# Hybrid SSD and gMLP diffusion step on one Trainium2 core: GpSimd casts the four upper parts of a weight tile first, then subtracts the four lower parts

## The reference: what is computed

```python
def _layer(x, mod, h0, lw, rows):
    ...
    h = rms_norm(x, norm_w) * (1 + scale[:, None]) + shift[:, None]
    proj = h @ w_in
    xbc_raw, z_m, dt_raw, u_raw, v_raw, z_g, gl_m, gl_g = jnp.split(
        proj, _split_points(IN_SIZES), axis=-1)
    y_m, h_fin = _ssd_branch(xbc_raw, dt_raw, z_m, h0, conv_w, conv_b, dt_bias, a_log,
                             d_skip, ssm_norm_w, rows)
    y_g = _gmlp_branch(u_raw, v_raw, z_g, sgu_ln_w, sgu_ln_b, w_sp, b_sp)
    merged = jax.nn.sigmoid(gl_m) * (y_m @ w_out_m) + jax.nn.sigmoid(gl_g) * (y_g @ w_out_g)
    return x + gate[:, None] * (merged @ w_out), h_fin
```

## Time and profile before

| what | value |
|---|---|
| median of 3 runs | 1401.03 us (1400.89 to 1401.64) |
| the profiled execution, its own time | 1401.26 us |
| its span in the trace | 1399.5 us |
| PE busy | 1387.0 us, 99% of the span |
| POOL busy | 1029.1 us, 74% of the span |
| DVE busy | 1027.1 us, 73% of the span |
| ACT busy | 467.1 us, 33% of the span |

### The profile page before, as it was taken

One profiled execution on the slowest core, in us unless ns is written; L12 is line 12 of the kernel. 1 busy time (PEld: TensorE's weight loads), 2 busy tenths in 40 slices (PEclk: granted clock), 3 DMA queues, 4 the chain that ended last, 5 costly groups with the idle time before them and its releaser, 6 DMA issues.

```text
span 1399.5 us, 27040 instructions
## 1 busy us (share of the span) xinstructions
PE 1387.0 (99%) x10101; PEld 1331.1 (95%) x10101; DVE 1027.1 (73%) x1503; ACT 467.1 (33%) x1039; POOL 1029.1 (74%) x1421
## 2 busy tenths in 40 slices
PE   8999999999999999999999999999999999999997
PEld 5899999999999999999998999999999999999997
DVE  6988679665677688999978766976566776869234
ACT  5432123214766333001252323241266661320122
POOL 3789886696554499998869898657765546979763
PEclk9999999999999999999999999999999999999999
DMA  9362665123766555444334455722346665453222
GB/s 366 126 151 76 191 167 159 61 66 127 188 179 192 177 204 212 150 151 155 106 136 122 107 165 149 192 86 61 106 135 191 193 173 201 139 190 120 76 76 91
DMA packets 198047, 206.85 MB, mean 148 GB/s; under 512 B 76592, under 2 KB 163760, under 8 KB 196784
## 3 DMA queue, kind: packets, MB, share of 16 engines
q1 hardware_dynamic: 116000, 155.13, 35.6%
q10 hardware_dynamic: 81936, 50.16, 12.4%
HBM read 179.23 MB, written 26.02 MB: 147 GB/s over the span
## 4 chain that ended last, share of the span: by engine, by line
PE 98%; DVE 1%; DMA 0%; SPq 0%; issue 0%; ACT 0%; DVEq 0%; ACTq 0%
PE acc L718 79%; PE X L684 5%; PE acc L684 3%; PE X L972 2%; PE X L952 2%; PE X L988 1%; PE X L1013 1%; PE acc L866 1%; PE X L981 1%; DVE p_lo L1606 1%; DMA ada_pre<-in_wada 0%; DVE ssq L1581 0%; PE X L825 0%; DVE xr L2143 0%; PE X L910 0%; PE acc L732 0%
## 5 line engine op out<-in xcount | busy, mean ns | idle before, releaser
L617 POOL CAST w_hi<-w_st 128x256 fp32r<-128x256 f32 x696 | 410.5, 604 | 337.1 <-PE acc L718 162.2
L621 POOL TENSOR_TENSOR w_lo<-w_st,w_hi 128x256 fp32r<-128x256 f32 x696 | 645.0, 936 | 0.0
L718 PE MATMUL acc<-h_hi,w_hi 128*128 128x320 f32 x1696 | 402.1, 318 | 0.0
L718 PE MATMUL acc<-h_lo,w_hi 128*128 128x320 f32 x1696 | 386.3, 309 | 0.0
L718 PE MATMUL acc<-h_hi,w_lo 128*128 128x320 f32 x1696 | 386.2, 309 | 0.0
L718 PEld LDWEIGHTS acc<-h_hi,w_hi 128*128 128x128 f32 x1696 | 284.4, 188 | 14.7 <-issue 11.8
L718 PEld LDWEIGHTS acc<-h_hi,w_lo 128*128 128x128 f32 x1696 | 283.5, 188 | 0.0
L718 PEld LDWEIGHTS acc<-h_lo,w_hi 128*128 128x128 f32 x1696 | 283.4, 188 | 0.0
L1824 DVE SCALAR_TENSOR_TENSOR cv<-raw,convw_sb,cv 128x642 f32<-128x642 f32 x128 | 137.2, 1072 | 4.5
L1540 DVE SCALAR_TENSOR_TENSOR ada_acc<-ada_st,sc,ada_acc 128x512 f32<-128x512 f32 x112 | 107.8, 1002 | 1.8
L1280 ACT ACTIVATE cvt<-cv 128x642 f32<-128x642 f32 x32 | 23.8, 744 | 158.1 <-DVE cv L1824 158.1
(11 more groups left out here) (264 smaller groups left out, 2322.5 us busy)
## 6 DMA issues: line engine op xcount, KB each, us to landing
w_st<-in_wts SPq DMA_DIRECT2D x174, 512.0 KB, 3.7
cum_bc<-cum_dram ACTq DMA_DIRECT2D x80, 256.0 KB, 5.0
ada_st<-in_wada SPq DMA_DIRECT2D x34, 512.0 KB, 4.3
ex_bc<-ex_dram ACTq DMA_DIRECT2D x64, 128.0 KB, 3.1
ada_pre<-in_wada SPq DMA_DIRECT2D x14, 512.0 KB, 8.9
xs<-xs_dram SPq DMA_DIRECT2D x64, 80.0 KB, 3.8
mga_dram<-c_buf SPq DMA_DIRECT2D x16, 320.0 KB, 5.2
xf<-xf_dram SPq DMA_DIRECT2D x4, 1280.0 KB, 7.1
```

Source lines behind the costliest of these rows:

```text
L617: nc.gpsimd.tensor_copy(quarter(w_hi, slot, q), quarter(w_st, slot, q)).then_inc(s_pool, 1)
L621: nc.gpsimd.tensor_tensor(quarter(w_lo, slot, q), quarter(w_st, slot, q), f(quarter(w_hi, slot, q)), ALU.subtract).then_inc(w_split, 1)
L718: last = mm(a[:, hf, 0:n1], w[:, s, cols], x[:, k, hf * HALF:hf * HALF + n1], start=(k == 0 and n == 0), stop=(k == KC - 1 and n == 2))
```

## The change

In GpSimd's loop the casts are no longer interleaved with the subtractions. Before, quarter q+1 was cast just ahead of the subtraction of quarter q; now all four quarters are cast and then all four are subtracted. The instructions, their operands and the counts on which the subtractions wait are the same.

```diff
         with pool.Fori(1, DEPTH * NT // 2) as i:
             for slot in range(2):
                 split(slot, 16 * i + 16, 2 * i + slot - 1)
-                split_hi(slot, 0)
                 for q in range(WQ):
-                    if q + 1 < WQ:
-                        split_hi(slot, q + 1)
+                    split_hi(slot, q)
+                for q in range(WQ):
                     split_lo(slot, q, 2 * WQ * i + (base + WQ * slot + q + 1))
```

## The result

The changed kernel takes 1403.32 us in the median of 20 runs, the kernel before 1401.17 us in 20 runs beside them. The ratio is 1.0016 with a 95% interval of 1.0010 to 1.0022: 2.15 us or about 0.16% slower. That is inside the 0.2% that the prediction called hard to tell from no change, and with 20 runs each it can be told.

What follows compares the result with a forecast made beforehand. PE's own stream was taken to bound the kernel, with GpSimd nowhere the bound. Waits of 0.43 + 0.13 + 0 + 0 = 0.56 us on the median 1401.03 gave 1401.6 us, range 1400.3 to 1403.5.

Steps and rivals of the forecast that it cites:

- the signs that it had set: In the changed trace: PE waits naming w_lo near 536 and 543 us, 0.3 to 0.7 us; mean split under 0.3 longer.
- PE bounds the kernel, and nothing can be gained: From 35 to 1391 us PE's gaps total 0.09 us; faster by over 0.2% (1398 us or less) had chance 0.03.
- What the order does to the four subtractions: First subtraction of a tile ends two casts later (0.7 to 1.9 us), second one cast; third, fourth unchanged; v tiles untouched.
- The waits at tiles 64 and 65: Near 536 and 543 us PE waits for late first subtractions, 0.43 and 0.13 us, together 0.56 us.
- Tiles 58 and 146, "just in time": First subtractions end 0.12 and 0.07 us ahead of PE's weight loads, so no wait; by the port rule 0.1 at 146.
- The rival "DVE is slowed": Last ym_lo ahead of tile 66: eight instructions at 0.35 us more, 2.8 against 7 us of room; no chance of its own.
- the high end: Waits at tiles 64, 65, 58, 146 of 0.56, 0.70, 1.65, 1.10 us, together 4.0; the range's end 1403.5 us.
- the second rival: Tiles 58 and 146 also wait: with the 0.56, 1.6 to 2.7 us; 1402.3 to 1403.8 us; chance 0.12.

Runs made afterwards that it cites:

- half_104_115: Changed kernel, but in tiles 104 to 115 each subtraction is cut into two of 128 columns: 1401.70 us against 1401.19 for the kernel before.
- alt_92_147: Changed kernel, but with casts and subtractions alternating as before for tiles 92 to 147: 1401.66 us against 1401.19 for the kernel before.
- double_58_146: Changed kernel, but one subtraction per two quarters in tiles 58, 59, 146 and 147: 1404.33 us against 1401.23 for the kernel before.
- grp_104_115: Kernel before, with casts grouped ahead of subtractions only for tiles 104 to 115: 1402.64 us against 1401.27 for the kernel before.
- alt_104_115: Changed kernel, but alternating casts and subtractions as before for tiles 104 to 115: 1402.09 us against 1401.27 for the kernel before.
- late_grouped: Changed kernel with PE's burst for unit 5 two chunks later in its tile: 1401.78 us against 1401.27 for the kernel before.
- its control: Kernel before (alternating) with PE's burst for unit 5 two chunks later: 1401.19 us against 1401.27 for the kernel before.

## Why the prediction was right, and where it was wrong

The sign and the range were right; the forecast of 1401.6 us was 1.7 us short, the loss was 2.15 us where the sum had 0.56, and its reason was not what happened. Of the signs that it had set, the mean split kept its length (5.85 us in both) and the time moved by less than 2.8 us, but between 35 and 1392 us no wait of a matmul names the subtraction: the only one listed is the 1.4 us at the burst.

- **PE bounds the kernel, and nothing can be gained: right for the time.** No variant is faster than the kernel before beyond its interval. The 0.09 us of gaps in PE was not all, though: the burst of unit 5 hid a wait of 0.26 us, and half_104_115, where DVE is early enough, gave back 0.3 us at that place.
- **What the order does to the four subtractions: right for the first, not quite for the third.** In its logic lo2 ends when it did. Counted from the start of its split it does in the mean over the 174 tiles (0.02 us earlier), but for single tiles it moves by 1.4 us forward to 2.0 us back. The DVE instructions that the eight meet are others, and in v tile 103, which had 0.32 us of room before its first matmul, it cost 0.34 us. The forecast left the v tiles out, "although they are the ones in which PE comes closest behind GpSimd", by counting instructions and not their turns with DVE. That this step goes with the alternating order is shown by alt_92_147; which DVE instruction made it was only read from the timeline (GpSimd's four subtractions take 3.42 us there beside `ex` and `xo` on DVE).
- **The waits at tiles 64 and 65, 0.43 and 0.13 us: they did not come.** The step that failed is "I take the tiles' own rows, since DVE's list is the same and is pinned to PE's tiles as before". The timelines of GpSimd and of DVE beside tile 64 in the changed kernel:

```profile
530.99 2.03 POOL L617 CAST w_hi<-w_st 128x256 fp32r<-128x256 f32 x4
532.98 5.16 POOL L621 TENSOR_TENSOR w_lo<-w_st,w_hi 128x256 fp32r<-128x256 f32 x4
```

```profile
534.89 1.36 DVE L1580 TENSOR_TENSOR ssq<-ssq,c_buf 128x640 f32<-128x640 f32 x1
```

  The split began 0.7 us earlier (530.99, before 531.68), and its four casts took 2.03 us, not 1.93 + 0.95 + 0.82: the last three are free, at 0.40 us each from 531.92 us on, where DVE is at an instruction that takes 0.82 us in both kernels (`c_buf<-c_buf,acc`). The first subtraction was done at about 534.3, not 536.66, and PE came at 536.4. DVE paid instead: the instruction at 534.89 started at 533.27 in the kernel before and took 1.01. There DVE has 7 us to spare before tile 66.
- **Tiles 58 and 146, "just in time": right in kind.** Tile 58 did not wait and tile 146 waited 0.16 us, for 0.07 us of room. The Trainium skill's rule that a two-input DVE instruction and GpSimd take turns ("SBUF — State Buffer", "Who interferes with whom"), by which the text had 0.1 us there, came closer than the rows alone. The way of pricing a late quarter holds: double_58_146 was expected to add 0.9 to 1.1 us to the changed kernel and added 0.95 by the medians.
- **The rival "DVE is slowed" was the cause, and it was given no chance.** The forecast had the mechanism right, word for word: DVE "now waits for a subtraction (0.70) where every second one waited for a cast (0.35)". It looked for its price at one place only, the last `ym_lo` ahead of tile 66, and found 7 us of room. The step that failed for the time as a whole is this one: the lateness of DVE was held against one hand-over only. It did not ask where else DVE hands something to PE with no room. That place was in the trace, at 897.80 against 897.91 us, and in the list of waits it is invisible. The runs with one part alone (grp_104_115, +1.4 us), one part undone (alt_104_115, 0.8 left), and the wait taken away with everything else kept (late_grouped, 0.5 left against 0.0 for its control) show this place to be worth 1.3 of the 2.15 us. The same burst in layer 0 is worth 0.35 more by the traces.
- **The range held by luck.** Its bounds were built for first quarters, and DVE's lateness happened to have a size that fell into them, 0.18 us under the high end. That end was itself added up too high. The high end and the second rival add tile 58's wait to those of tiles 64 and 65, but from tile 58's first cast to 549 us GpSimd waits for nobody, so a PE that is late since tile 58 would have found tile 64 ready. Without this the high end is 1.65 + 1.10 = 2.75 us in place of 4.0, and the second rival 1.1 to 2.2 us in place of 1.6 to 2.7. A range that took in 2.2 us would have ended at 1403.2, short of the 1403.32 measured. (The rival's 1402.3 us doesn't follow from its 1.6 either, which gives 1402.6.)

Why DVE meets more subtractions is shown in its numbers (48 short taps for 64, subtractions dearer by 48 ns and casts cheaper by 45) but argued in its reason: a split begins when PE frees a slot, and then DVE is often between two jobs. In the kernel before, the first two casts of a tile each took 0.54 us in the mean over the 174 tiles and the last two 0.65 and 0.68. Grouping moves all casts into this quiet start and leaves the subtractions for the time when DVE is at work. No run moved DVE's work against the split to test it.

## What to carry to other kernels

When GpSimd and DVE both read SBUF, reordering GpSimd can change how long DVE's instructions take, even though neither does more work: here a two-input DVE instruction waits until the GpSimd instruction that it finds at work has ended, so what counts is which kind it finds there, and short ones are kinder to it. Price such a change on both engines. And look for the places where an engine hands over just in time: compare the end of what PE reads with PE's start, because a hand-over 0.1 us ahead of that start shows as no wait at all until something moves. Compare PE's start also with the beat of the matmuls ahead of it, since a wait of up to a quarter of a microsecond hid behind their drawn ends.

## What was not expected of the hardware

The turns of DVE and GpSimd are whole instructions to a close measure, but a DVE instruction doesn't pay for the whole of the one that it finds. A convolution tap of 642 columns takes 0.89 us when GpSimd does nothing at all, as this one in the changed kernel, which lies in the 1.89 us that GpSimd waits for PE:

```profile
L1823 DVE SCALAR_TENSOR_TENSOR cv<-raw,convw_sb,cv x1: 886/886/886, 892.2 to 892.2; 128x642 f32<-128x642 f32 x1
```

```profile
893.67 2.79 POOL L617 CAST w_hi<-w_st 128x256 fp32r<-128x256 f32 x4 [1.89 <-PE acc L717]
```

Behind a cast of 256 columns a tap takes the same (0.90 us), behind a subtraction of 128 columns 0.97, of 256 columns 1.25 and of 512 columns 1.81. Typically these GpSimd instructions end 0.22, 0.28, 0.56 and 1.12 us after the tap has started, and in the last three cases each tap ends 0.68 or 0.69 us behind the end of the GpSimd instruction. So the first 0.2 us of a tap pass beside GpSimd's instruction for nothing, and only what GpSimd still needs beyond that is added: nothing for a cast, 0.08, 0.35 and 0.91 us for the subtractions. That is why DVE loses time where subtractions take the place of casts beside it.

The other surprise is that a GpSimd instruction which waits on a semaphore that its own engine's last instruction raises starts 0.12 us later than one that doesn't (0.47 against 0.35 us from start to start), four times for each tile; in the stretch without slack, tiles 58 to 66, PE lost 1.6 us in the run that had it.
